# Gated scan: GpSimd folds a unit's score planes ahead of the forget gates' work of the same iteration

## The chip, the cores and the metric

The kernel runs on one core of a Trainium2 chip as one launch. The metric is the device time of an execution in microseconds. A core has TensorE (PE in the profile, PEld for its weight loads), VectorE (DVE), ScalarE (ACT), GpSimd (POOL) and SyncE (SP, which issues DMAs here). Each takes its own instructions in order and waits for others by semaphores.

## The reference, cut to what matters

The program is two model blocks in float32, one after the other. The change lies in one branch of the second block, a gated linear attention in two directions over 256 context tokens and 512 latent tokens, with 4 heads of 128 channels:

```python
def hgrn_forget(z, lb):
    log_f = jax.nn.log_sigmoid(z) + jnp.log1p(lb * jnp.exp(-z))
    k = (1.0 - lb) * jax.nn.sigmoid(-z)
    return k, log_f

def step(s, inp):                       # gla_chunk_scan, one chunk
    qi, ki, vi, fi = inp
    a = jnp.cumsum(fi, axis=2)
    o_inter = jnp.einsum('bhtd,bhde->bhte', qi * jnp.exp(a), s)
    diff = a[:, :, :, None, :] - a[:, :, None, :, :]
    decay = jnp.exp(jnp.where(tri, diff, NEG_BIG))
    scores = jnp.einsum('bhtd,bhjd,bhtjd->bhtj', qi, ki, decay)
    o_intra = jnp.einsum('bhtj,bhje->bhte', scores, vi)
    a_last = a[:, :, -1, :]
    s_new = (jnp.exp(a_last)[..., None] * s
             + jnp.einsum('bhjd,bhje->bhde', ki * jnp.exp(a_last[:, :, None, :] - a), vi))
    return s_new, o_inter + o_intra
```

The rest of the program (the first block with its own attention, recurrence and experts, the two attentions of the second block, its merge and feed-forward part) surrounds it and isn't touched.

## The kernel before, in words

`gated_scan` is one stage: each engine has a program of its own in it, and all meet at its end. It takes tiles of 128 tokens. A **round** r is one tile of each direction d: rounds 0 and 1 are the context, rounds 2 to 5 the latents. The forget gates of rounds 0 to 2 are made in the stage's first part. Then a loop runs over 32 **units** (s, d, h): step s of the latents, direction, head, so that eight units make up a round. The decay within a tile is taken apart into eight planes (`level`, `spans`), so that the scores of a unit are eight products of 128x128, which are masked and added up.

All engines run the loop over iterations i, each at its own pace:

- TensorE (lines 3258 to 3320): in some iterations a look-ahead (`look_ahead`, L3231) and in the next one a turn (`turn`, L3237, four transposes of the new keys); then `sum_spans(i)` (L3269), `pair(i - 1)` (L3285, eight products) and `move(i - 2)` (L3299 to L3302), which uses the four folded planes of its unit and adds to the state. `move` waits for `folded`.
- ScalarE (L3372 on): the exponentials of `sum_spans(i)` into `c_e` (L3380), and its part of the forget gates: `soften` (L3326, L3328), `logs` (L3332, L3334), `place` (L3343) and `rate` (L3338). Exponentials and logarithms need different tables, so table loads stand between them.
- VectorE (L3453 on): `c_xq` (L3462), the masking of unit i - 1's eight planes out of PSUM into `g` (L3471), `c_xk` (L3476), in some iterations `keep_turned` (L3416) and `weigh` (L3412), its part of the forget gates (`prepare` L3402, `soft_end` L3406), and for unit i - 2 the state (L3494) and the output (L3499 or L3501).
- GpSimd (L3200 to L3215): its part of the forget gates, and `fold(i - 1)` (L3192), which adds planes 4 to 7 of `g` onto planes 0 to 3. `g` has two buffers, named gate_w (even units) and c_gm (odd units) in the profile.

The forget gates of rounds 3, 4 and 5 are made inside the loop. `forget_at(i)` gives for an iteration the phase p, the round r and the direction d with 8 (r - 3) + p + d = i. Phase 0 is `prepare` on VectorE and `limit` on GpSimd (L3172), phase 1 `soften` on ScalarE and `raise_` on GpSimd (L3176), phase 2 `logs`, phase 3 `soft_end` on VectorE and `join` on GpSimd (L3181 and L3183, two operations), phase 4 `place` and `rate` on ScalarE, phase 5 `shrink` on GpSimd (L3187). So of every eight iterations the first seven have some of this work. The look-ahead of direction 0 of the next round comes in the sixth (iterations 5, 13, 21) and waits for `place`; the turn comes in the seventh (6, 14, 22) and waits for `shrink`. Those of direction 1 follow four iterations later.

The order of the work on every engine is written out by hand; nothing plans it. GpSimd issues no DMA in this loop.

Of the kernel before, what the change touches and what calls it, by code (L numbers as in the profile page):

```python
# [3067 lines left out]
def gated_scan(k, a, t, w_in, hl, q, lf, v, yc, cg, gate_w, gate_w_in, first_w, close_in):  # L3068
# [41 lines left out]
    def soft_of(r, d):  # L3110
        return (xq[r][:, 4 * d:4 * d + 4, :].rearrange("p h n -> p (h n)") if r < AHEAD else k_of(r, d))

    def lift_of(r, d):
        return (e[r][:, 4 * d:4 * d + 4, :].rearrange("p h n -> p (h n)") if r < AHEAD else lift[:, d, :])
# [4 lines left out]
    def z_of(r, d):  # L3119
        return lf[d][:, tile_of(r, d), :]  # L3120

    def k_of(r, d):
        return kc[r % 3][d][:, :]
# [10 lines left out]
    def forget_at(i):  # L3134
        return [(p, r, d) for r in range(AHEAD, ROUNDS) for d in D2 for p in range(6) if 8 * (r - AHEAD) + p + d == i]
    turn_at = {i + 1: rd for i, rd in ahead_at.items()}
    with k.stage("spans_in", "bound_in", "wcg_in0", "wcg_in1", "gate_made", "gate_kept", "q_ready", "prepared",
# [11 lines left out]
        @block.sync  # L3149
        def _(sp):  # L3150
            sp.dma_start(ring[1][:, :, :], w_in[:, :, 3584 + P:3584 + 2 * P]).then_inc(wcg_in[1], 16)
            sp.dma_start(bound[:, 0, :, :], k.bounds[0][None, :, :].to_broadcast([P, 2, 512])).then_inc(bound_in, 16)
            sp.dma_start(bound[:, 1, :, :], k.bounds[1][None, :, :].to_broadcast([P, 2, 512])).then_inc(bound_in, 16)
            for d in D2:
                sp.dma_start(after[d][:, :], a["k_after"][d]).then_inc(spans_in, 16)
                sp.dma_start(spans[d][:, :, :], a["k_spans"][d]).then_inc(spans_in, 16)
                sp.dma_start(level[d][:, :, :], a["k_level"][d]).then_inc(spans_in, 16)
            for m in range(2, 4):
                sp.wait_ge(gate_made, m - 1)
                sp.dma_start(ring[m % 2][:, :, :], w_in[:, :, 3584 + m * P:3584 + (m + 1) * P]  # L3160
                             ).then_inc(wcg_in[m % 2], 16)
            sp.wait_ge(spans_in, 96)
            sp.wait_ge(summed, 2 * 2 * H)
            sp.dma_start(first_w, w_in[:, :, 4096:4096 + 256]
                         ).then_inc(close_in[0], 16)

        @block.gpsimd
        def _(gp):
            chain = Chain(gp, pool)

            def limit(r, d):
                gp.tensor_scalar(lift_of(r, d), z_of(r, d), -44.0, None, ALU.max).then_inc(limited, 1)  # L3172

            def raise_(r, d):
                gp.wait_ge(lift_exp, 2 * r + d + 1)
                gp.tensor_tensor(lift_of(r, d), lift_of(r, d), bound[:, 0, d, :], ALU.mult).then_inc(lifted, 1)  # L3176

            def join(r, d):
                gp.wait_ge(soft_out, 2 * r + d + 1)
                gp.wait_ge(lift_log, 2 * r + d + 1)  # L3180
                gp.tensor_tensor(lift_of(r, d), soft_of(r, d), lift_of(r, d), ALU.add).then_inc(joined, 1)  # L3181
                gp.wait_ge(joined, 2 * (r - AHEAD) + d + 1)
                gp.tensor_tensor(k_of(r, d), soft_of(r, d), z_of(r, d), ALU.subtract).then_inc(kc_log, 1)  # L3183

            def shrink(r, d):
                gp.wait_ge(kc_exp, 2 * r + d + 1)
                gp.tensor_tensor(k_of(r, d), k_of(r, d), bound[:, 1, d, :], ALU.mult).then_inc(kc_made, 1)  # L3187

            def fold(i):
                gp.wait_ge(g_kept, i + 1)  # L3190
                m = g[i % 2]
                gp.tensor_tensor(m[:, 0:4, :], m[:, 0:4, :], m[:, 4:8, :], ALU.add).then_inc(folded, 1)  # L3192
            gp.wait_ge(bound_in, 32)
            for r in range(AHEAD):
                for d in D2:
                    raise_(r, d)
            for r in range(AHEAD):
                for d in D2:
                    shrink(r, d)
            for i in range(N + 1):  # L3200
                for p, r, d in forget_at(i):
                    if p == 0:
                        if r > AHEAD:
                            gp.wait_ge(lf_made, 2 * r)
                        limit(r, d)
                    elif p == 1:
                        raise_(r, d)
                    elif p == 3:
                        join(r, d)
                    elif p == 5:  # L3210
                        shrink(r, d)
                if i:
                    fold(i - 1)

        @block.tensor  # L3215
        def _(pe):
# [1057 lines left out]
```

## Time and profile before

| | |
|---|---|
| median of 3 runs | 3472.3 us (3465.14 to 3481.37) |
| profiled execution | 3473.43 us |
| its span | 3471.3 us |
| TensorE busy | 3054.5 us (88%) |
| VectorE busy | 1751.9 us (50%) |
| ScalarE busy | 864.6 us (25%) |
| GpSimd busy | 484.4 us (14%) |

The span is from the first to the last instruction that the profiler saw, and the execution's time is what the runs measure too. Busy shares are means over stages of very different kinds, so what a change in one stage is worth is read from that stage.

### The profile page before, as it was taken

How to read it: one execution, taken by the hardware profiler on the slowest of the kernel's cores; microseconds unless marked ns; L12 is line 12 of the kernel's file. 1: busy time of each engine (PE TensorE's matmuls, PEld its weight loads, DVE VectorE, ACT ScalarE, POOL GpSimd, SP SyncE). 2: the span in 40 equal slices, each digit the busy share in tenths (PEclk: the TensorE clock that was granted, in tenths of full speed). 3: DMA queues.
4: the chain of work that ended last, by engine and by line, in shares of the span. 5: the costliest groups of instructions: out<-in, count | busy, mean ns of one | idle time of the engine just before them, and what ended most of it. 6: DMA issues, size and time to landing. Idle time of an engine off the chain costs nothing. (4 is left out here: it accounts for less than half of the span.)

```text
span 3471.3 us, 65159 instructions
## 1 busy us (share of the span) xinstructions
PE 3054.5 (88%) x27070; PEld 2341.6 (67%) x27070; DVE 1751.9 (50%) x3124; ACT 864.6 (25%) x1794; POOL 484.4 (14%) x731
## 2 busy tenths in 40 slices
PE   6899899968757998999688759899998899899998
PEld 3676798744436775897554434576666688788887
DVE  3445576431133445675511154355477776577742
ACT  3123233031121223331211141233444210122210
POOL 0000552011110003550011120000055200000000
PEclk9998899979978997999889979999999999999999
DMA  7110301089983103102399981101100122222220
GB/s 250 46 37 29 148 4 60 29 324 379 401 278 103 46 19 129 49 4 87 127 362 388 399 242 43 51 25 31 57 1 13 61 73 98 85 73 85 82 91 34
DMA packets 173515, 420.15 MB, mean 121 GB/s; under 512 B 31361, under 2 KB 117761, under 8 KB 148017
## 3 DMA queue, kind: packets, MB, share of 16 engines
q1 hardware_dynamic: 154257, 382.05, 29.8%
q0 software_dynamic: 8736, 17.32, 2.1%
q10 hardware_dynamic: 10240, 16.79, 1.5%
q8 instruction: 206, 3.38, 0.4%
q14 instruction: 76, 0.62, 0.1%
HBM read 399.38 MB, written 50.54 MB: 130 GB/s over the span
## 5 line engine op out<-in xcount | busy, mean ns | idle before, releaser
L2179 PE MATMUL ps<-e_w,e_xt 128*64 128x256 f32 x1792 | 232.5, 417 | 69.1 <-DMA e_w<-in_moe_w 68.4
L2179 PEld LDWEIGHTS ps<-e_w,e_xt 128*64 128x64 f32 x1792 | 153.5, 151 | 170.3 <-issue 85.8
L776 PE MATMUL ps<-h,win 128*128 128x264 f32 x960 | 229.3, 393 | 16.6 <-DVE pad L945 15.0
L2286 DVE TENSOR_TENSOR e_hid<-ps,e_silu 64x256 f32<-64x256 f32 x64 | 39.4, 616 | 400.4 <-ACT e_silu L2245 400.4
L776 PEld LDWEIGHTS ps<-h,win 128*128 128x128 f32 x960 | 182.6, 193 | 53.1 <-issue 22.2
L1559 DVE COPY_PREDICATED inv<-level,ps 124x480 f32<-124x480 int32 x144 | 100.6, 699 | 71.8 <-PE ps L1463 71.8
L3710 PE MATMUL ps<-h_lat,wt 128*128 128x256 f32 x528 | 127.8, 384 | 6.7 <-ACT h_lat L3847 6.5
L3710 PE MATMUL ps<-h_lat,w_sums 128*128 128x256 f32 x544 | 130.8, 384 | 0.0
L2198 PE MATMUL ps<-e_w,e_hid_t 128*64 128x512 f32 x448 | 113.8, 627 | 16.9 <-DMA e_w<-in_moe_w 12.0
L2249 ACT ACTIVATE e_hid_t<-ps 128x128 f32<-128x128 f32 x64 | 17.8, 278 | 406.3 <-PE ps L2187 406.3
L1463 PE MATMUL ps<-inv,nt 60*60 60x60 f32 x2880 | 112.4, 218 | 5.5 <-issue 4.5
L3710 PEld LDWEIGHTS ps<-h_lat,wt 128*128 128x128 f32 x528 | 101.1, 192 | 23.2 <-issue 7.3
L3710 PEld LDWEIGHTS ps<-h_lat,w_sums 128*128 128x128 f32 x544 | 105.1, 193 | 14.8
L3815 ACT ACTIVATE part<-ps 128x256 f32<-128x256 f32 x54 | 20.7, 384 | 364.5 <-PE ps L3710 267.9
L1390 ACT ACTIVATE nt<-ps 124x240 f32<-124x240 f32 x180 | 66.8, 371 | 170.1 <-PE ps L1452 163.6
L3710 PE MATMUL ps<-y_branch,wt 128*128 128x256 f32 x448 | 107.7, 379 | 0.8 <-ACT ff_up L3855 0.8
L1452 PE MATMUL ps<-inv,by 60*60 60x60 f32 x2880 | 100.2, 221 | 6.5 <-DVE inv L1552 3.8
L945 DVE COPY pad<-ps 128x264 f32<-128x264 f32 x60 | 26.0, 433 | 150.2 <-PE ps L776 150.2
L1463 PEld LDWEIGHTS ps<-inv,nt 60*60 60x60 f32 x2880 | 96.9, 135 | 6.4 <-issue 4.7
L1452 PEld LDWEIGHTS ps<-inv,by 60*60 60x60 f32 x2880 | 88.7, 135 | 13.1 <-DVE inv L1552 4.7
L2918 PE MATMUL ps<-wc,h_lat 128*128 128x256 f32 x384 | 91.5, 383 | 6.0 <-DVE log_f L3029 4.8
L1460 PE MATMUL ps<-nt,inv 60*60 60x60 f32 x2304 | 89.9, 218 | 5.8 <-issue 4.9
(668 smaller groups left out, 6657.8 us busy)
## 6 DMA issues: line engine op xcount, KB each, us to landing
e_w<-in_moe_w SPq DMA_DIRECT2D x168, 1024.0 KB, 13.8
early<-in_moe_w SPq DMA_DIRECT2D x24, 1024.0 KB, 12.1
wt<-in_w_up SPq DMA_DIRECT2D x22, 1024.0 KB, 4.9
y_rows<-e_y ACTq DMA_DIRECT2D x128, 128.0 KB, 7.1
win<-in_w_in SPq DMA_DIRECT2D x10, 1536.0 KB, 6.7
wmod<-in_w_mod SPq DMA_DIRECT2D x24, 512.0 KB, 15.8
wt<-in_w_in SPq DMA_DIRECT2D x11, 1024.0 KB, 4.9
early<-in_w_mod SPq DMA_DIRECT2D x16, 512.0 KB, 11.3
```

Of the source, the lines that this page charges most:

```text
L776: last = pe.matmul(ps[:, 7, 0:HT], lhsT=ring[(s + 1) % 2][:, i, o:o + P], rhs=k.h[:, i, h * HT:(h + 1) * HT], start=(i == 0), stop=(i == K ...
L945: dve.tensor_copy(pad[:, 1 + h * HT:1 + (h + 1) * HT], ps[:, 7, 0:HT]).then_inc(emptied, 1)
L1390: act.activation(nt[z][:, :, :], ps[0:R, bank_a(c), 0:RT * WC].rearrange("p (f n) -> p f n", f=RT), ACT.Copy).then_inc(x_kept[z], 1)
L1452: last = pe.matmul(ps[hw, a0, f * WC:(f + 1) * WC], lhsT=by[b][z][hw, f, 0, :], rhs=inv[z][hw, 0, f, :], start=True, stop=True)
L1460: pe.matmul(ps[hw, a0, f * WC:(f + 1) * WC], lhsT=inv[z][hw, 1, f, :], rhs=nt[z][hw, f, :], start=True, stop=True)
L1463: last = pe.matmul(ps[hw, a0, (RT + f) * WC:(RT + f + 1) * WC], lhsT=nt[z][hw, f, :], rhs=inv[z][hw, 1, f, :], start=True, stop=True)
L1559: dve.copy_predicated(inv[z][0:R, :, :, :], k.level[0:R, level, d:d + 2, None, :].to_broadcast([R, 2, RT, WC]), ps[0:R, a0, 0:2 * RT * WC] ...
L2179: last = pe.matmul(ps[half, 2 + z, 0:EH], lhsT=xt[z][:, f, :], rhs=w[:, f, :], start=(f == 0), stop=(f == KD - 1))
L2198: last = pe.matmul(ps[half, 4 + z, :], lhsT=hid_t[z][:, t, :], rhs=m2[:, t, q * 512:(q + 1) * 512], start=(t == 0), stop=(t == 1))
L2286: dve.tensor_tensor(hid[z][high, :].rearrange("s (t q) -> s q t", t=2), ps[high, 2 + z, 0:EH].rearrange("s (q t) -> s q t", t=2), si[z][hi ...
L2918: last = pe.matmul(ps[:, 7, 0:cols], lhsT=lhsT, rhs=rhs, start=(i == 0), stop=(i == KD - 1))
L3710: last = pe.matmul(out, lhsT=w[:, i, :], rhs=x[:, i, :], start=(i == 0), stop=(i == w.shape[1] - 1))
```

## The change

In GpSimd's loop the fold of unit i - 1 is moved from behind the forget gates' work of iteration i to ahead of it. Its wait for the planes (`g_kept`) moves with it. No instruction is added or taken out, and no other engine's program changes.

```diff
             for i in range(N + 1):
+                if i:
+                    fold(i - 1)
                 for p, r, d in forget_at(i):
                     if p == 0:
                         if r > AHEAD:
@@
                         join(r, d)
                     elif p == 5:
                         shrink(r, d)
-                if i:
-                    fold(i - 1)
```

## Rows read from the trace of the kernel before

**Rows 1.** The page: the span, and the chain that ended last by engine.
```profile
span 3471.3 us, 65159 instructions
PE 20%; DVE 1%; ACT 0%; issue 0%; DVEq 0%
```
**Rows 2.** Windows of a round and after a gap: us; busy (count) PE, PEld, DVE, ACT, POOL; clock; DMA.
```profile
2593.00:2644.40 51.40, 45.85 (x271) 35.14 (x270) 39.16 (x49) 21.72 (x34) 29.01 (x18) 0.93 0.07 22
...
2612.00:2615.00 3.00, 3.00 (x8) 1.59 (x7) 0.94 (x3) 0.15 (x1) 2.44 (x2) 0.50 0.00 0
```
**Rows 3.** Waits, 2593 to 2644.3 us, then 2540 to 2740 us: total, times, longest.
```profile
PE ps L3299 <- POOL c_gm L3192: 5.3, 2, 2.7
...
PE ps L3299 <- POOL c_gm L3192: 17.3, 7, 2.8
```
**Rows 4.** Timeline of TensorE: start, us, instruction, [idle before <-releaser].
```profile
2610.85 0.49 PE L3299 MATMUL ps<-c_xq,c_state 128*128 128x128 f32 x2 [2.72 <-POOL c_gm L3192]
...
2612.58 3.27 PE L3269 MATMUL ps<-spans,log_f 128*128 128x512 f32 x4
2615.69 1.73 PE L3285 MATMUL ps<-c_xq,c_xk 128*128 128x128 f32 x14
...
2617.47 0.39 PE L3299 MATMUL ps<-c_xq,c_state 128*128 128x128 f32 x2
...
2618.82 1.02 PE L3231 MATMUL ps<-log_f,after 128*128 128x512 f32 x2
2619.68 1.88 PE L3269 MATMUL ps<-spans,log_f 128*128 128x512 f32 x4
...
2625.92 0.79 PE L3299 MATMUL ps<-c_xq,c_state 128*128 128x128 f32 x2 [2.58 <-POOL c_gm L3192]
...
2628.64 0.79 PE L3237 MATMUL ps<-ident,k_c 128*128 128x128 f32 x4
```
**Rows 5.** Timeline of GpSimd.
```profile
2590.80 1.49 POOL L3172 TENSOR_SCALAR fg_lift<-log_f 128x512 f32<-128x512 f32 x1
2593.71 2.04 POOL L3192 TENSOR_TENSOR c_gm<-c_gm 128x512 f32<-128x512 f32 x1 [1.42 <-DVE c_gm L3471]
...
2608.54 2.26 POOL L3192 TENSOR_TENSOR c_gm<-c_gm 128x512 f32<-128x512 f32 x1
2612.48 1.27 POOL L3181 TENSOR_TENSOR fg_lift<-k_c,fg_lift 128x512 f32<-128x512 f32 x1 [1.68 <-DVE k_c L3406]
...
2623.62 2.25 POOL L3192 TENSOR_TENSOR c_gm<-c_gm 128x512 f32<-128x512 f32 x1
2625.83 2.17 POOL L3187 TENSOR_TENSOR k_c<-k_c,fg_bound 128x512 f32<-128x512 f32 x1
```
**Rows 6.** Timeline of VectorE.
```profile
2591.03 1.46 DVE L3462 TENSOR_TENSOR c_xq<-c_e,c_q 128x1024 f32<-128x1024 f32 x1 [0.87 <-ACT c_e L3380]
2592.41 1.21 DVE L3471 TENSOR_TENSOR c_gm<-ps,level 128x1024 f32<-128x1024 f32 x1
...
2594.54 1.75 DVE L3402 SCALAR_TENSOR_TENSOR k_c<-log_f 128x512 f32<-128x512 f32 x1
...
2603.81 1.21 DVE L3471 TENSOR_TENSOR c_gm<-ps,level 128x1024 f32<-128x1024 f32 x1
...
2610.72 1.07 DVE L3476 TENSOR_TENSOR c_xk<-c_e,k_t 128x896 f32<-128x896 f32 x1
...
2622.71 2.03 DVE L3462 TENSOR_TENSOR c_xq<-c_e,c_q 128x1024 f32<-128x1024 f32 x1 [1.28 <-ACT c_e L3380]
```
**Rows 7.** Timeline of ScalarE.
```profile
2610.86 1.28 ACT L3379 ACT_TABLE_LOAD   x1
...
2616.86 0.63 ACT L3343 ACTIVATE log_f<-fg_lift 128x512 f32<-128x512 f32 x1
...
2621.66 1.02 ACT L3380 ACTIVATE c_e<-ps 128x1024 f32<-128x1024 f32 x1
```

## The prediction

> **What bounds the kernel now.** I read the page first, for the span and for the chain that ended last [rows 1]. That chain is followed back only over the last fifth of the span, all of it in the closing stage, so it says nothing of the gated scan. The scan's stage lies at about 2524 to 2740 us, and all engines meet at its end, so a microsecond on the scan's own path is a microsecond of the span. Which engine that path runs through comes from three further views of the stage.
>
> The windows [rows 2] show a round of eight iterations (eight units of the scan, the forget gates of one tile pair beside them) with TensorE busy 45.85 of 51.40 us, VectorE 39 and GpSimd only 29. TensorE is the bound, and it has gaps. The waits [rows 3] name them: TensorE waits 5.3 us in this round, in two pieces, for GpSimd's fold of c_gm, 17.3 us in 7 pieces over all four rounds. Six of the seven belong to the three rounds that carry forget work, two in each; the seventh is the last unit's, where nothing is queued ahead of the fold. The timelines of the engines show the mechanism. Write S, P and M for TensorE's three pieces of an iteration (span sums, the eight pair products, and the move that reads the folded planes), A and T for look-ahead and turn, and number units from 0. The planes of unit 9 are written by VectorE at 2605.02 (2603.81 + 1.21 [rows 6]), but their fold starts at 2608.54 [rows 5], behind the raise of iteration 10, which waits for ScalarE's table loads. M(9) starts at 2610.85 after 2.72 us of idleness [rows 4]. Unit 11's fold stands likewise behind a join until 2623.62, and M(11) starts at 2625.92 after 2.58 us. The second cost is the clock. The granted clock is 0.50, the 1.2 GHz level, over 2612 to 2615 [rows 2], right after the first gap: S(12) takes 3.27 us where S(13) at the full 2.4 GHz takes 1.88, so 1.39 us is lost there and, with M(9) taking 1.73 (2612.58 - 2610.85) where M(10) takes 1.35 (2618.82 - 2617.47), 1.8 us in all. After the second gap M(11) takes 2.72 (2628.64 - 2625.92), which is 1.4 more than 1.35. So the two late folds cost 5.3 + 1.8 + 1.4 = 8.5 us a round, some 25.5 us in three rounds, 0.7% of the span.
>
> **The change part by part.** No instruction is added or removed. In each of the 32 iterations that fold, GpSimd now meets the wait for that iteration's planes first and does the forget work behind it. Iterations of the last round and every eighth one have no forget work; there nothing changes. There are no DMAs in GpSimd's queue here, and SP's queue waits only for S(15), to load a first weight of the next stage.
>
> *Removed.* Both waits of M for a late fold: 5.3 us a round. The fold that follows its planes at once is ready in time: g(7) ends at 2593.62, the fold behind it runs 2593.71 to 2595.75 [rows 5, 6], that is 2.13 us after the planes, while TensorE still owes P (1.78 us, 2617.47 - 2615.69 [rows 4]), which starts about 1.1 us after the planes. M would come at 2.9 us, so 0.8 us are spare.
>
> *Added: collisions of GpSimd with VectorE.* A two-input operation of GpSimd takes 1.27 us alone (join, 2612.48) and 2.04 when it starts during VectorE's product for xk (fold, 2593.71); VectorE's prepare that then waits takes 1.75, and an xq product that meets two GpSimd operations takes 2.03 [rows 5, 6] where the equally large g takes 1.21. One waits while the other runs. Folding first puts every fold on xk and moves the forget work from the quiet time at the start of an iteration onto the next xq.
>
> The skill has a rule that is harsher than these rows. "SBUF — State Buffer", in "SBUF: two separate sides" of the Trainium skill, has VectorE and GpSimd take an exclusive lock for a whole instruction. The limit at 2590.80 runs 1.49 us [rows 5], and the xq that starts 0.23 us into it takes 1.46 [rows 6], 0.25 more than 1.21; by the rule it would wait 1.26 us. So by the row a displaced limit costs 0.25 us and by the rule about 1.3, and with two limits in each of three rounds the rule would add about 6 us.
>
> *Added: the forget chain is later behind its fold.* TensorE doesn't only need folds. A of iteration 13 needs the new log gates, which come by VectorE's soft end, GpSimd's join (two operations), ScalarE's place; and T of iteration 14 needs GpSimd's shrink of iteration 13. I walk one round, in us after 2600, the time of before in brackets.
> - M(9) no longer waits for its fold. VectorE is some 0.5 late by collisions, P(10) starts at 6.6 (6.1), VectorE's output copies end at 8.9, so M(9) runs 8.9 to 10.25 (10.85 to 12.58), S(12) from 10.25 (12.58). Gain so far 2.3.
> - P(11) needs xk(11), which ends at 11.79 [rows 6], or with one more collision at 12.8. It was not late before, because S(12) was. ScalarE's table load up to 12.14 [rows 7] holds e(12) back to 13.2 whatever TensorE does. These two take 0.9 us of the gain.
> - The fold of unit 10 now stands before the join. It waits out xk(11) and runs 12.75 to 14.0; the soft end waits for it, to 14.6; the join's first operation runs to 15.9; the waiting xq(12) to 17.05; the join's second to 18.25; ScalarE's place (0.63 [rows 7]) to 18.9. A(13) starts at 18.95 (18.82). TensorE, done with M(10) at 16.5, idles 2.45 us. If none of these collide, the join ends at 15.5 and A starts at 16.2: 2.6 us early.
> - T(14) hangs on S(13) now. S start to end of e 3.0 (2619.68 to 2622.68 [rows 4, 7]), xq 1.2, g 1.2, fold 2.13 after g, shrink about 1.25: 8.85 us with latencies, where S, P and M are 4.85 of work. Before it was 8.96 (2628.64 - 2619.68 [rows 4]), spent on the late fold and the low clock. The wait of 2.6 us for a fold is thus replaced by one of about 4 us for the shrink: the shrink is in the same iteration as the fold and is now behind it. Without collisions T(14) is at 16.2 + 0.86 + 8.85 = 25.9, 2.7 early; with them (xq(13) held 0.75 by the join of iteration 12) at 18.95 + 0.86 + 0.75 + 8.85 = 29.4, 0.8 late.
> - From T(14) on the round is as before, but for the clock.
>
> Between -2.7 and +0.8 I take 0: the rows show a collision each time two such operations meet, but not each meeting need fall as in my walk.
>
> *The clock.* A gap of 2.6 or 2.7 us was followed by the low level both times. Now the gaps are 2.45 before A(13) and 4 before T(14). At the low level A and S(13) lose 0.4 + 1.4 = 1.8, T and S(14) 0.2 + 1.4 = 1.6. The bounds are 0 and 3.4; part of the low time may fall into the longer gap, and a late S(13) spares the collision of 0.75. I take 1.5.
>
> Sum: 3 rounds x (0 + 1.5) = +4.5 us, between 3 x (-2.7) = -8 and 3 x (0.8 + 3.4) = +12.6. The profiled execution took 3473.4 us (span 3471.3), 1.1 above the median of 3472.3, so the forecast is 3473.4 + 4.5 = 3478 for that execution and 3477 against the median.
>
> **The rivals.**
> *The waits go and nothing takes their place.* Price -25.5 us, 3447. For it: the waits are real, and GpSimd is busy little more than half the round. Against it: the shrink stands behind a fold whose planes need S of the same iteration; only the order in the queues decides that, not anybody's speed. It would take a T that isn't waiting. From 17.4 us, 5.8 a round, it counts as faster. Chance 0.06.
> *The low clock multiplies: slower.* The wait for xk(11), the wait before A(13) and the one before T(14) each bring a whole low stretch at 1.8, 1.8 and 1.6 us, and all collisions stand: 0.8 + 5.2 = 6.0 a round, +18, 3490. It decides from 5.8 a round. For it: three gaps where there were two. Against it: the gap before P(11) is 0.9 us, a third of those that a low stretch followed, and the wait before T(14) swallows delays of TensorE that don't sit on S(13). Chance 0.07.
> *The displaced limits block wholly.* The four others stand as forecast and each limit costs 1 us more on the path: 4.5 + 6 = +10.5, 3483. Two limits a round meet an xq. Against it stands the 1.46 us row. By the skill's rule named above this would be the case. Chance 0.08.
>
> **How the numbers follow.** The forecast has 0.79. Its time, 3477, is within 0.5% (17.4 us), which is about what a measurement of this kernel can tell from no change: its three runs lie 16 us apart. The range holds the bounds -8 and +12.6 around the median and some 4 to 5 us of scatter of a median: 3461 to 3490, which takes in the third rival and the edge of the second. Faster 0.06 (first rival), slower 0.07 (second), same 0.87.
>
> **What would show it.** In the changed profile TensorE's waits for the c_gm fold should be gone but for the last unit's. In their place the turn (L3237) should wait for the shrink (L3187) for about 4 us once in each of three rounds, and the look-ahead (L3231) for ScalarE's place (L3343) for up to 2.5. Folds should average 2 us and more, both buffers alike. Two low stretches a round should remain, moved to A and T. A round should take 51 to 54 us. The prediction is wrong if T(14) follows M(12) with no gap, if rounds are below 48 us, or if the clock stays at 1.0 across those gaps.

## The result, and the profile after

The changed kernel takes 3477.9 us (median of 20 runs) against 3470.2 us of the kernel before (20 runs beside it): the ratio is 1.0023, 95% interval 1.0014 to 1.0031. That is 7.7 us slower, where 4.5 us was forecast (3477). It is within 0.5%, as the chances had it, but the interval excludes zero. The profiled execution took 3477.7 us, its span is 3475.8.

The scan's loop, from the first S to the end of the last M, took 201.3 us in the trace of before (2537.99 to 2739.32) and takes 208.6 now (2537.31 to 2745.92): 7.3 us more, about the difference of the medians. (The spans of the two profiled executions differ by 4.5 us only: outside this loop the second one was 2.8 us shorter, which is no more than the scatter from run to run.)

The waits of the stage (line waited for, total, times, longest), to be read against [rows 3]:

```profile
PE ps L3237 <- POOL k_c L3187: 12.0, 3, 4.3
...
PE ps L3231 <- ACT log_f L3343: 6.7, 3, 2.2
...
PE ps L3299 <- POOL c_gm L3192: 1.3, 1, 1.3
```

The 17.3 us for late folds have shrunk to the 1.3 of the last unit, which was there before. In their place stand 12.0 us for the shrink and 6.7 us for the place, together 18.7: a wait that is 16.0 us smaller at one door is 18.7 us longer at two others.

The timeline of TensorE in the second round (start, length, instruction, idle time before). Its iteration 9 begins 1.14 us later than before (look-ahead at 2594.12, before at 2592.98), so 1.14 is to be taken off when a start is laid beside [rows 4]:

```profile
2594.12 1.02 PE L3231 MATMUL ps<-log_f,after 128*128 128x512 f32 x2
...
2609.69 0.46 PE L3299 MATMUL ps<-c_xq,c_state 128*128 128x128 f32 x2 [0.19 <-DVE y_branch L3499]
...
2611.10 1.88 PE L3269 MATMUL ps<-spans,log_f 128*128 128x512 f32 x4
2613.48 1.83 PE L3285 MATMUL ps<-c_xq,c_xk 128*128 128x128 f32 x14 [0.49 <-DVE c_xk L3476]
...
2619.52 1.10 PE L3231 MATMUL ps<-log_f,after 128*128 128x512 f32 x2 [2.24 <-ACT log_f L3343]
2620.46 1.88 PE L3269 MATMUL ps<-spans,log_f 128*128 128x512 f32 x4
...
2629.74 1.09 PE L3237 MATMUL ps<-ident,k_c 128*128 128x128 f32 x4 [4.28 <-POOL k_c L3187]
2630.61 3.62 PE L3269 MATMUL ps<-spans,log_f 128*128 128x512 f32 x4
2634.03 2.17 PE L3285 MATMUL ps<-c_xq,c_xk 128*128 128x128 f32 x14
...
2648.06 1.02 PE L3231 MATMUL ps<-log_f,after 128*128 128x512 f32 x2
```

M(9) starts 2.3 us earlier than before, A(13) 0.4 earlier, and T(14) at the very time of before (2629.74 - 1.14 = 2628.60 against 2628.64 [rows 4]). S(14) then runs at half the clock. The round takes 53.94 us instead of 51.37. GpSimd's timeline shows why T waits: the fold can't start before its planes, and the shrink is behind it.

```profile
2626.33 2.04 POOL L3192 TENSOR_TENSOR gate_w<-gate_w 128x512 f32<-128x512 f32 x1 [2.29 <-DVE gate_w L3471]
2628.33 1.26 POOL L3187 TENSOR_TENSOR k_c<-k_c,fg_bound 128x512 f32<-128x512 f32 x1
```

ScalarE's rate had the shrink's input ready at 2619.89 (start 2619.28 and 0.61 us), and GpSimd was idle for 2.29 us ahead of that fold: the shrink could have run there. The windows of TensorE's gap and of what follows it, columns as in [rows 2]:

```profile
2626.00:2629.00 3.00, 0.00 (x0) 0.00 (x0) 1.71 (x4) 0.00 (x0) 2.67 (x2) 0.85 0.00 0
2630.00:2634.00 4.00, 4.00 (x8) 1.96 (x7) 0.00 (x0) 0.00 (x0) 0.00 (x0) 0.50 0.00 0
```

And the groups of the stage that collide (busy, mean ns):

```profile
L3462 DVE TENSOR_TENSOR c_xq<-c_e,c_q 128x1024 f32<-128x1024 f32 x32 | 49.1, 1536 | 40.6 <-ACT c_e L3380 40.6
...
L3192 POOL TENSOR_TENSOR gate_w<-gate_w 128x512 f32<-128x512 f32 x16 | 32.7, 2047 | 53.7 <-DVE gate_w L3471 53.7
L3192 POOL TENSOR_TENSOR c_gm<-c_gm 128x512 f32<-128x512 f32 x16 | 31.7, 1980 | 42.6 <-DVE c_gm L3471 42.4
```

All folds now take 2 us; gate_w's were 1.61 on average before. The xq products went from 1.36 to 1.54.

### The profile page after: what moved, and what is told of

It is laid out like the page before. It is cut to its first block and busy times, and to the rows that moved or that the text cites. A ratio compares the mean times of both kernels' runs of the same rounds, so it can differ in the third digit from the quotient of the medians.

```text
span 3475.8 us, 65159 instructions
## 1 busy us (share of the span) xinstructions
PE 3052.5 (88%) x27070; PEld 2337.1 (67%) x27070; DVE 1764.6 (51%) x3124; ACT 864.8 (25%) x1794; POOL 495.3 (14%) x731
```

## The experiments

All ratios are to the kernel before, run beside them. "Stage" is the loop as above: 201.3 before, 208.6 in the changed kernel.

| kernel | ratio, 95% interval | median us | stage us |
|---|---|---|---|
| shrink ahead of the fold | 0.9966 (0.9953 to 0.9979) | 3460.8 | 191.3 |
| join and shrink ahead | 0.9999 (0.9987 to 1.0010) | 3469.8 | 200.3 |
| gap before the turn filled | 1.0010 (0.9998 to 1.0022) | 3472.0 | 201.4 |
| short fold | 0.9985 (0.9973 to 0.9998) | 3464.8 | 194.8 |
| look-ahead and turn late | 0.9959 (0.9944 to 0.9973) | 3459.0 | 186.1 |
| kernel before, both late | 1.0017 (1.0004 to 1.0029) | 3475.3 | 206.1 |
| both late, xk first | 0.9976 (0.9964 to 0.9988) | 3461.9 | 192.4 |
| changed kernel, xk first | 1.0061 (1.0044 to 1.0077) | 3491.2 | 218.8 |
| turn alone late | 0.9973 (0.9959 to 0.9988) | 3460.4 | 190.6 |
| both late, shrink ahead | 0.9954 (0.9937 to 0.9971) | 3452.2 | 184.7 |

**Is it the shrink's place in the queue?** GpSimd's loop with the shrink alone ahead of the fold:

```diff
             for i in range(N + 1):
+                for p, r, d in forget_at(i):
+                    if p in (5,):
+                        join(r, d) if p == 3 else shrink(r, d)
                 if i:
                     fold(i - 1)
...
-                    elif p == 3:
+                    elif p == 3 and p not in (5,):
                         join(r, d)
-                    elif p == 5:
-                        shrink(r, d)
```

> The changed kernel, but with GpSimd's shrink ahead of the fold of its iteration (the shrink doesn't depend on that fold's planes); raise, limit and join stay behind the fold. Theory 1 (order in the queue: the turn of iteration 14 waits only because the shrink stands behind a fold whose planes need the same iteration's S): the shrink runs right after the join of the iteration before, T(14) comes about 3.3 us earlier, its gap falls from 4.3 to about 1 us, no low stretch follows, and a round falls from 53.9 to about 48.3 us: 17 us below the changed kernel, 9 below the kernel before, ratio to it 0.997. Theory 2 (the loss is the collisions of GpSimd's and VectorE's two-input operations, which this edit leaves): the turn's wait turns into another wait further on, and the time stays within 3 us of the changed kernel, ratio to before 1.002.

Measured: ratio 0.9966, 17 us below the changed kernel's median. The timeline of TensorE (lines are one further down in this kernel) has the turn right behind M, and GpSimd's has the shrink ahead of the fold:

```profile
2628.33 0.39 PE L3303 MATMUL ps<-v_c,k_c 128*128 128x128 f32 x2
2628.55 0.60 PE L3238 MATMUL ps<-ident,k_c 128*128 128x128 f32 x4
2628.99 1.88 PE L3270 MATMUL ps<-spans,log_f 128*128 128x512 f32 x4
```

```profile
2625.54 1.27 POOL L3187 TENSOR_TENSOR k_c<-k_c,fg_bound 128x512 f32<-128x512 f32 x1
2629.18 2.04 POOL L3192 TENSOR_TENSOR gate_w<-gate_w 128x512 f32<-128x512 f32 x1 [2.37 <-DVE gate_w L3472]
```

The folds are as long as in the changed kernel (2.04 and 1.98 us on average), so the collisions of the folds are all there, and the time fell all the same: theory 2 falls. One thing was not foreseen: the look-ahead's wait of 2.24 us, unchanged, was here followed by the low level in two of three rounds, with S(13) at 3.2 us. The round shown takes 48.7 us for 48.3 expected.

**And the join as well?** Both stand ahead of the fold instead of behind it:

```diff
+                for p, r, d in forget_at(i):
+                    if p in (3, 5):
+                        join(r, d) if p == 3 else shrink(r, d)
                 if i:
                     fold(i - 1)
...
-                    elif p == 3:
+                    elif p == 3 and p not in (3, 5):
                         join(r, d)
-                    elif p == 5:
-                        shrink(r, d)
```

> The changed kernel, but with both the join and the shrink ahead of the fold, so that the fold is moved only past raise and limit. It takes away the fold ahead of the look-ahead's chain too. Theory 1: place and look-ahead come about 1 us earlier, but M(10) waits some 3.7 us for its fold behind the join, with a low stretch after it; no wait of the turn is left. A round of about 49.3 us, 14 us below the changed kernel, ratio to before 0.998, thus no better than with the shrink alone ahead. Theory 2 (collisions): within 3 us of the changed kernel.

Measured: 0.9999, where 0.998 was expected: right that it is worse than the shrink alone, wrong by some 6 us in size (a round of 51.3 us for 49.3). The wait is where it was expected but longer and dearer:

```profile
2625.46 0.80 PE L3300 MATMUL ps<-c_xq,c_state 128*128 128x128 f32 x2 [4.24 <-POOL gate_w L3192]
...
2627.75 0.64 PE L3303 MATMUL ps<-v_c,k_c 128*128 128x128 f32 x2
2628.18 1.91 PE L3232 MATMUL ps<-log_f,after 128*128 128x512 f32 x2
2629.89 2.48 PE L3270 MATMUL ps<-spans,log_f 128*128 128x512 f32 x4
```

M took 2.72 us and A 1.71 at the low level, and S a part more. So the join must not stand ahead of the fold: it waits for VectorE's soft end, which comes after the planes anyway.

**What does the clock cost?** Four products more in TensorE's gap:

```diff
                     pe.wait_ge(ahead_exp, 2 * r + d + 1)
+                    if i in (6, 14, 22):
+                        for _ in range(4):
+                            pe.matmul(ps[:, 7, :], lhsT=after[d][:, :],
+                                      rhs=spans[d][:, 0:4, :].rearrange("p l n -> p (l n)"), start=True, stop=True)
                     turn(r, d, 7)
```

> The changed kernel with four more 128x512 products (0.86 us each at the full clock, 3.4 us in all) put into the gap ahead of the turn of iterations 6, 14 and 22; they write the bank that the turn overwrites, and the output is the same. They fill the wait of 4.3 us without lengthening the chain. If the low stretch after that wait is what makes the change slower than the order alone would (theory 1: about 2.35 us a round), T stays where it is and S(14) takes 1.9 instead of 3.6 us: 7 us below the changed kernel, ratio to before 1.000. If the low clock comes from something other than that gap, S(14) stays at 3.6 us and the time is that of the changed kernel, ratio 1.002.

Measured: 1.0010, the stage at 201.4, 7.2 us below the changed kernel's 208.6. By the ratios the two are 4.5 us apart, and their intervals overlap, so the reading rests on the trace. It shows T at its old place and S(14) at the full clock (L3316 are the added products):

```profile
2635.07 3.70 PE L3316 MATMUL ps<-spans,after 128*128 128x512 f32 x8 [0.34 <-ACT c_ahead L3398]
2638.90 0.66 PE L3237 MATMUL ps<-ident,k_c 128*128 128x128 f32 x4
2639.40 1.88 PE L3269 MATMUL ps<-spans,log_f 128*128 128x512 f32 x4
```

From A(13) (2628.79) to T(14) are 10.11 us, in the changed kernel 10.22. So the work in the gap delays nothing, and with it no low stretch followed any of the three turns. From the turn to the next look-ahead the three rounds take 16.19 us each, in the changed kernel 17.79, 18.32 and 18.56: 6.1 us in all. Another 0.9 of the 7.2 us doesn't come from the filling: the look-ahead's wait in the first round, which was followed by a low stretch in the changed kernel's trace, was not here, and it lies ahead of the first added product. Without low stretches the changed kernel's stage is that of the kernel before: the waits of the two kernels, with the low stretches that before had, come to the same length.

**Are the collisions the cause?** A fold of one of four plane pairs; three quarters of its addition are left out:

```diff
-                gp.tensor_tensor(m[:, 0:4, :], m[:, 0:4, :], m[:, 4:8, :], ALU.add).then_inc(folded, 1)
+                gp.tensor_tensor(m[:, 0:1, :], m[:, 0:1, :], m[:, 4:5, :], ALU.add).then_inc(folded, 1)
```

> The changed kernel, but each fold adds only one of its four plane pairs (three quarters of the fold's addition are left out, so the output is not the reference's). The fold then takes some 0.35 us of its own instead of 1.27. Theory 1 (the order in the queue makes the waits, the collisions only lengthen them): a fold still waits out the xk product, but ends about 0.9 us earlier; the look-ahead's chain gains 0.9 and the turn's another 0.9 us a round, the turn still waits about 3.3 us for the shrink, with its low stretch. A round of about 52 us, 5 to 6 us below the changed kernel, ratio to before 1.0005. Theory 2 (collisions are the cause): with the collisions three quarters gone the waits of look-ahead and turn go too, rounds below 49 us, ratio 0.997 or less.

Measured: 0.9985, 13 us below the changed kernel where 5 to 6 were expected. The waits are as theory 1 had them:

```profile
PE ps L3237 <- POOL k_c L3187: 9.2, 3, 3.1
...
PE ps L3231 <- ACT log_f L3343: 5.5, 3, 1.8
```

The waits have not gone. In the second round they are 1.2 and 0.4 us shorter, and T(14) comes 33.1 us after A(9) instead of 35.6, 2.5 earlier for 1.8 expected. How much of that is collision is not shown: a fold takes 1.2 us instead of 2.0 on average and still waits for the xk product, so what it lost is its own addition, and soft end and prepare, which wait for a fold, went from 1.76 and 1.58 us to 0.94 and 0.90. That collisions are not the cause rests on the shrink ahead, which leaves them, more than on this run. The second round (2591.67 to 2640.74) takes 49.07 us, because here the wait of 3.07 us was not followed by a low stretch and S(14) took 1.88; in the other two rounds it was (3.14 and 3.54 us). That share of the gain is the clock's.

**Is fold-first good once nothing waits for the shrink?** Look-ahead and turn of direction 0 one iteration later, in the changed kernel and in the kernel before:

```diff
-    ahead_at = {8 * (r - CT) + 4 * d - 3: (r, d) for r in range(CT, ROUNDS) for d in D2 if (r, d) != (CT, 0)}
+    ahead_at = {8 * (r - CT) + 3 * d - 2: (r, d) for r in range(CT, ROUNDS) for d in D2 if (r, d) != (CT, 0)}
```

> The changed kernel with look-ahead and turn of direction 0 one iteration later (6, 14, 22 and 7, 15, 23 instead of 5, 13, 21 and 6, 14, 22), still before their results are needed. Theory 1: both replaced waits (2.24 us of the look-ahead for place, 4.28 us of the turn for the shrink) and the low stretch (2.35) go; small waits for xk remain: a round of about 46 us, 24 us below the changed kernel and 16 below the kernel before, ratio 0.995. Theory 2 (collisions bind): VectorE's own chain is then the bound, rounds of 50 us and more, at most 12 us below the changed kernel.

> The kernel before (fold behind the forget work), but with look-ahead and turn of direction 0 one iteration later, as in e5_late_turn. Theory 1: in the kernel before TensorE is late by the two late folds and waits neither for place nor for the shrink, so moving look-ahead and turn brings nothing: rounds of 51 to 52 us, ratio 1.000. Together with e5_late_turn (0.996) it gives what fold-first is worth once nothing waits for the shrink: about 14 us. If the late turn alone brings the gain of e5 (rival: the order of fold and forget work is indifferent), the ratio here is 0.996 as well.

Measured: 0.9959 (0.995 expected) and 1.0017 (1.000 expected). The two kernels differ only in the place of the fold, as the pair of this study does, and here fold-first makes the kernel 0.6% or 20 us faster, where about 14 were expected (stage 186.1 against 206.1 us). The waits that remain in the first, and in the second:

```profile
PE ps L3285 <- DVE c_xk L3476: 8.7, 14, 1.4
```

```profile
PE ps L3299 <- POOL c_gm L3192: 22.2, 7, 4.2
```

The second one's slowing was not expected. In its second round M(9) to M(11) take 15.03 us (2621.32 to 2636.35) and took 15.07 before. Its S(12) ran at the full clock after M(9)'s late fold, unlike before, and the time so saved came back as a longer wait for the fold of unit 11 (4.24 us, before 2.58): that fold's join is bound to VectorE's soft end and collides with xq(13) (join 2.13 us, fold 2.16). The look-ahead, which stood in that time before, then comes on top behind it. In the other two rounds the fold of the later unit was waited for just as long (4.23 and 4.22 us), though S(4) and S(20) took 3.33 and 2.75 us there, so the full clock of S(12) is at most part of the reason.

**VectorE's order.** To take the fold off the xk product, VectorE makes xk before it masks the planes, with late look-ahead and turn, and in the changed kernel as it is:

```diff
+                if i < N:
+                    s, d, h = units[i]
+                    dve.tensor_tensor(xk[i % 2][:, :, :], e[i % 3][:, 0:7, :],
+                                      k_t[s % 2][d][:, h:h + 1, :].to_broadcast([P, 7, P]),
+                                      ALU.mult).then_inc(operands, 1)
                 if 1 <= i <= N:
...
                                      ALU.mult).then_inc(g_kept, 1)
-                if i < N:
-                    s, d, h = units[i]
-                    dve.tensor_tensor(xk[i % 2][:, :, :], e[i % 3][:, 0:7, :],
-                                      k_t[s % 2][d][:, h:h + 1, :].to_broadcast([P, 7, P]),
-                                      ALU.mult).then_inc(operands, 1)
```

> As e5_late_turn, and VectorE makes xk before it masks the planes instead of after. The pair products then get xk 1.2 us earlier, and the fold no longer starts into the xk product. In e5 a round took 46.65 us with some 1.9 us of waits for xk. Theory 1: these go, and what stays is TensorE's work and ScalarE's table loads: rounds of about 45 us, 5 us below e5, ratio to before 0.9945. If the collisions come back on another VectorE operation (the fold meeting prepare, soft end, or the next xq), the round stays at 46 us or more and the ratio at 0.996.

> The changed kernel with only the order of xk and the masking exchanged on VectorE (look-ahead and turn stay where the changed kernel has them). Theory 1: the planes come 1 us later and the fold is 0.8 us shorter, so the chain S, e, xq, xk, mask, fold, shrink keeps its 8.9 us and the turn still waits about 4 us, with the low stretch; only the 0.5 us waits for xk go, about 1 us a round: 3 us below the changed kernel, ratio to before 1.001. Theory 2 (the collision of fold and xk is the cause): the turn's wait falls by more than 2 us, rounds below 51 us, ratio 0.999 or less.

Measured: 0.9976 (0.9945 expected) and 1.0061 (1.001 expected); both expectations failed, and for a reason that stands in the code. P writes the same two banks that the masking empties (`g_kept` in `pair`), so the masking, not xk, is what the next P now waits for (with both late; L3476 is the masking in this kernel):

```profile
2613.17 1.88 PE L3269 MATMUL ps<-spans,log_f 128*128 128x512 f32 x4
2616.00 1.80 PE L3285 MATMUL ps<-c_xq,c_xk 128*128 128x128 f32 x14 [0.95 <-DVE c_gm L3476]
```

The folds did get shorter (1.41 and 1.39 us on average with both late), and it brought nothing: the collisions came back on xk, which takes 1.42 us on average for 1.08, and 2.15 beside a join or a shrink. In the changed kernel with xk first, the waits of look-ahead and turn were 3.36 and 3.7 us in the second round and that round took 57.8 us. In all three rounds a low stretch followed each of the two (S at 2.5 to 3.6 us).

**The two replaced waits apart, and whether the cures add up.** The turn alone one iteration later (its edit is below), and both late with the shrink ahead of the fold:

```diff
-    turn_at = {i + 1: rd for i, rd in ahead_at.items()}
+    turn_at = {i + 2 - rd[1]: rd for i, rd in ahead_at.items()}
```

> The changed kernel with only the turn of direction 0 one iteration later (7, 15, 23); the look-ahead stays in iterations 5, 13, 21. It parts the two replaced waits. Theory 1: the turn waits for nothing (-4.3 us a round and its low stretch), the look-ahead still waits 2.24 us for place. From the rounds of 46.65 us with both late: 46.65 + 2.24, and 0 to 1.7 for a low stretch, some 49.5 us, the stage at 194 us against 186 with both late and 208.6 in the changed kernel; ratio to before 0.998. It should equal the kernel with the shrink ahead of the fold (stage 191.3, ratio 0.9966) within some 3 us, since both only free the turn.

> Look-ahead and turn late as in e5_late_turn, and the shrink ahead of the fold as in e1_shrink_ahead. Theory 1: the shrink's place in the queue matters only through the turn's wait, which the late turn has already taken away, so the two don't add up: the stage stays at 186 us, ratio to before 0.996. If the two gains came from different causes (the rival: e1 gains by fewer collisions), they would add up to some 200 - 14 - 10: a stage near 176 us and a ratio of 0.993.

Measured: 0.9973 and 0.9954. The turn alone late gives a stage of 190.6 (194 expected), that of the shrink ahead being 191.3: two different edits that both free the turn are worth the same. The look-ahead's share is the rest to 186.1. Shrink ahead on top of both late changes the stage by 1.4 us (184.7), so the cures don't add up, as one cause demands. This last has the lowest median of the study, 16 us below the kernel before and some 24 below the changed one, though its interval overlaps that of both late alone.

## Why the prediction was right

*The removed waits: right.* Forecast 5.3 us a round and all but the last unit's gone; they are. M(9) was forecast at 8.9 and came at 8.6 (2609.69 - 1.14, in us after 2600).

*The walk through the forget chain: right, on its hindered side.* P(11) forecast 12.8 with its collision, came at 12.3; A(13) 18.95, came at 18.4, with an idle time of 2.24 for 2.45; T(14) between 25.9 and 29.4 with 28.6 taken, came at 28.6 after 4.28 us of waiting for "about 4". S(13) to T(14) took 9.28 us (2620.46 to 2629.74), the 8.85 of the walk and 0.4 of the collision with the join (xq(13) 1.63 us for 1.2). In the other two rounds the turn came at its old time too, within 0.1 us. That the sum is so near the 0 taken is partly luck: A came 0.4 us early, S to T took 0.3 longer than before, and the prediction chose 0 between -2.7 and +0.8 without a row that fixed it. That the wait moves to the shrink because of its place in the queue, and not for lack of speed, is shown by the shrink ahead and by the turn alone late (17 us less than the changed kernel each).

*The collisions: right in kind.* The third rival, a displaced limit that blocks an xq wholly, did not appear. In the changed kernel xq(9) started 0.2 us before the end of a limit and took 1.23 us. A clearer row stands in the kernel with both late and xk first, where an xq started 0.48 us into a limit, ran beside the rest of it and was not longer either:

```profile
2593.14 1.49 POOL L3172 TENSOR_SCALAR fg_lift<-log_f 128x512 f32<-128x512 f32 x1
...
2593.62 1.23 DVE L3462 TENSOR_TENSOR c_xq<-c_e,c_q 128x1024 f32<-128x1024 f32 x1 [1.13 <-ACT c_e L3380]
```

The Trainium skill's rule of a lock for the whole instruction ("SBUF — State Buffer", "SBUF: two separate sides") would make that xq wait 1.0 us, so it does not hold for this pair. The other way round the limit does wait: one that started during an xq took 2.46 us (2604.15 in the changed kernel). For GpSimd's two-input operations the rule agrees with the trace: soft end takes 1.76 us behind a fold, where it took 0.68 before, and a fold that meets xk 2.0 for 1.27.

*The clock: the term that was too small.* Taken at 1.5 us a round; in the second round T, S(14) and P lost 0.4 + 1.7 + 0.4 = 2.6 us (T to S 0.87 for 0.44, S to P 3.42 for 1.72, P to M 2.22 for 1.78). The prediction priced T and S(14) at 1.6 us: its 1.4 for S came from S(12) of before, which took 3.27 us where S(14) took 3.62, and P was not in it. The forecast held that the low stretch would partly fall into the longer gap. The clock did fall a little before its end (0.85 over 2626 to 2629), but the stretch after it was full. On the other side, of the two low stretches a round that were forecast only the turn's came each time; the look-ahead's came in the first round alone. The three rounds grew by 1.8, 2.6 and 2.9 us, 7.3 in all, for 3 x 1.5; the third, 54.2 us, is just above the 51 to 54 forecast for a round. The filled gap shows that the low stretches behind the turns make up 6.1 us of it.

*The rivals.* The first (the waits go and nothing takes their place, 3447) would have needed a turn that isn't waiting; with that given, more than half of it happens: the stages of the kernels with both late are 15 and 17 us below that of the kernel before, for the 25.5 of the rival. The price of the second (three low stretches a round, 3490) is met by the changed kernel with xk first, 3491, but not its mechanism: there it is two stretches and longer chains. In the changed kernel the 0.5 us waits for xk brought no low stretch.

## What to carry to other kernels

When an operation is moved ahead in an in-order queue, what it waits for becomes what everything behind it waits for: list all that stands behind, and for each who needs it and when. Here the fold was late behind work that it didn't need, and moving it ahead made work late that didn't need the fold; the answer was to part the phases (the shrink, whose input was long ready, ahead of the fold, the join, which waits for a late input, behind it) or to ask for their results one iteration later. Whether a reordering is good can depend on the place of its reader: the same edit changed the time by +0.2% with look-ahead and turn in one iteration and by about -0.6% with them in the next.

## What the runs showed of the hardware that was not expected

The same idle time of TensorE is not always followed by the low clock. A wait of 2.24 us for the place was followed by it in one of three rounds of the changed kernel and of the one with the turn alone late, in two of three with the shrink ahead, in none with the gap before the turn filled. Waits of 2.6 to 2.8 us for a fold were followed by it six times out of six in the kernel before, but one of 2.71 us with both late was not. One of 3.07 us (short fold) was in two of three, and those of 4.2 to 4.3 us each time. Nor is the price the same: behind the changed kernel's three turns it was 1.7, 2.6 and 2.9 us (T, S and P together). So it can't be read off the length of one gap. Four otherwise useless products in the gap ahead of each turn, which cost no time, took it away there.

The limit and VectorE's products exclude each other only in part. An xq that started 0.23 us into a limit took 0.25 us more [rows 6], one that started 0.48 us into it took no more, and a limit that started during an xq took 2.46 us instead of 1.49.
